# A two-layer mixture-of-experts trunk: expert rows added by gathers into SBUF in place of accumulating scatters into DRAM

## What is computed

```
x = _layer_norm(DEEPNORM_ALPHA * x + mixed, ln_g[l, 0], ln_b[l, 0])
x = _layer_norm(DEEPNORM_ALPHA * x + grouped_moe(x, w_router, b_router, w_e_in[l], w_e_out[l]),
                ln_g[l, 1], ln_b[l, 1])

def grouped_moe(x, ...):              # T = 1024 tokens of D = 1024
    expert, weight = two experts of each token, with weights that sum to 1
    order = jnp.argsort(flat_e)       # the 2048 (token, expert) pairs sorted by expert
    xs = xt[order // TOP_K]
    h_gate, h_up = jnp.split(lax.ragged_dot(xs, w_e_in, group_sizes), 2, axis=-1)
    y = lax.ragged_dot(jax.nn.silu(h_gate) * h_up, w_e_out, group_sizes)
    y = y * weight.reshape(-1)[order][:, None]
    out = jnp.zeros_like(xt).at[tok].add(y)
```

## Time and profile before

| | |
|---|---|
| median of 3 runs | 3053.19 us (3050.14 to 3059.01) |
| the profiled execution, its own time | 3060.01 us |
| its span | 3058.3 us |
| mean granted TensorE clock | 0.953 |
| busy PE / DVE / ACT / POOL | 91% / 51% / 38% / 10% of the span |
| DMA | 398.58 MB, mean 130 GB/s |

### The profile page before, as it was taken

The page is one execution under the profiler, slowest core; times in us unless marked ns, Lnnn a source line. Parts: engine busy times, 40 slices in busy tenths (PEclk is TensorE's granted clock), DMA queues, the critical chain, the costliest instruction groups (busy, mean ns, idle before and its releaser), DMA issues.

```text
span 3058.3 us, 47623 instructions
## 1 busy us (share of the span) xinstructions
PE 2796.5 (91%) x15876; PEld 1463.5 (48%) x15877; DVE 1561.2 (51%) x2494; ACT 1163.7 (38%) x1846; POOL 309.4 (10%) x240
## 2 busy tenths in 40 slices
PE   5999999999999599999579999999999995999994
PEld 3555554554444345454345555555544442454542
DVE  3243473343346667656633345634433466577665
ACT  3234413222222157655432444132222321577663
POOL 0000000000000023222310000000000000132323
PEclk8999999999999799999789999999999996999996
DMA  7200001111115389977722000111111154699974
GB/s 256 70 1 29 29 18 36 52 35 53 52 62 185 126 301 347 323 257 240 221 88 70 28 1 29 35 35 35 53 49 46 58 207 154 222 340 360 314 255 143
DMA packets 150903, 398.58 MB, mean 130 GB/s; under 512 B 13700, under 2 KB 58928, under 8 KB 149904
## 3 DMA queue, kind: packets, MB, share of 16 engines
q1 hardware_dynamic: 133104, 327.59, 29.5%
q0 software_dynamic: 14816, 54.12, 7.1%
q10 hardware_dynamic: 2816, 14.68, 1.3%
HBM read 343.91 MB, written 56.63 MB: 131 GB/s over the span
## 4 chain that ended last, share of the span: by engine, by line
PE 77%; DVE 6%; issue 6%; PEld 3%; DMA 3%; ACT 2%; DVEq 2%; SPq 1%; POOL 0%; PEldq 0%; ACTq 0%; POOLq 0%
PE PA L2031 15%; PE PA L1606 10%; PE PA L1608 10%; PE PA L1607 10%; PE PB L2050 7%; PE PC L1587 3%; PE PB L1608 3%; PE PB L1607 3%; PE PB L1606 3%; PE PD L1606 2%; PE PD L1608 1%; PE PD L1607 1%; DMA W<-in_w_in_dram 1%; PE PA L1704 1%; PEld PA L1606 1%
## 5 line engine op out<-in xcount | busy, mean ns | idle before, releaser
L2031 PE MATMUL PA<-XT,RA 128*128 128x512 f16 x2304 | 511.2, 382 | 9.6 <-DVE RA L1023 6.3
L1606 PE MATMUL PA<-XT,W 128*128 128x512 f16 x1216 | 461.7, 380 | 0.7 <-issue 0.7
L1607 PE MATMUL PA<-XT,W 128*128 128x512 f16 x1216 | 461.3, 379 | 0.0
L1608 PE MATMUL PA<-XT,W 128*128 128x512 f16 x1216 | 461.2, 379 | 0.0
L2031 PEld LDWEIGHTS PA<-XT,RA 128*128 128x128 f16 x2304 | 226.2, 98 | 276.9 <-issue 15.6
L1023 DVE SCALAR_TENSOR_TENSOR XT<-OT,XT 128x1024 f16<-128x1024 f32 x256 | 295.0, 1219 | 40.4 <-ACT XT L901 40.3
L1023 DVE SCALAR_TENSOR_TENSOR W<-W 128x512 f16<-128x512 f32 (+2 forms) x320 | 199.6, 660 | 167.3 <-ACT W L675 155.7
L825 ACT ACTIVATE WK<-PA,bT 128x512 f32<-128x512 f32 x128 | 87.9, 687 | 495.9 <-PE PA L1608 495.4
L2050 PE MATMUL PB<-W,WK 128*128 128x512 f16 x1152 | 260.8, 384 | 6.7 <-DVE W L1023 4.4
L901 ACT ACTIVATE XT<-OT 128x1024 f16<-128x1024 f32 x240 | 230.7, 1043 | 44.1 <-issue 40.9
L1252 DVE SCALAR_TENSOR_TENSOR MKV<-WK,PB 128x512 f32<-128x512 f32 x96 | 66.0, 688 | 339.2 <-PE PB L1608 339.2
(11 more groups left out here) (355 smaller groups left out, 4239.1 us busy)
## 6 DMA issues: line engine op xcount, KB each, us to landing
OT<-in_w_e_in_dram SPq DMA_DIRECT2D x256, 512.0 KB
RA<-in_w_e_out_dram SPq DMA_DIRECT2D x128, 512.0 KB
W<-in_w_in_dram SPq DMA_DIRECT2D x104, 512.0 KB, 4.7
W<-in_w_branch_dram SPq DMA_DIRECT2D x32, 256.0 KB, 4.9
W<-in_w_out_dram SPq DMA_DIRECT2D x16, 512.0 KB, 5.2
x_rows<-RC SPq DMA_DIRECT2D x16, 512.0 KB, 5.5
y_sum<-RC SPq DMA_DIRECT2D x16, 512.0 KB, 5.9
OT<-y_sum SPq DMA_DIRECT2D x16, 512.0 KB, 3.7
```

What stands on the lines that cost most here:

```text
L1606: mm(dst, lhs(0), rhs(0), start=first, stop=False)
L1607: mm(dst, lhs(0), rhs(1), start=False, stop=False)
L1608: return mm(dst, lhs(1), rhs(0), start=False, stop=last)
L2031: q = mm(PA[:, half, :], ROWS[:, a, k * P:(k + 1) * P], EIS[:, b, k, half * HALF:(half + 1) * HALF], start=k == 0 and a + b == 0, stop=k = ...
```

## The change

- y_sum goes. A DRAM tensor y_rows with one place per slot (32 tiles of 128 rows) takes its place. POOL stores each tile of YROW whole and plainly (store_tile), without a column of indices.
- SP no longer stores x1 into y_sum, and no longer loads x2 from it.
- x2 is now x1's own buffer (RC). After the last store has landed, POOL issues two indirect gathers with an add for each token tile, from y_rows into x2: the first expert's rows (j = 0) and the second's (j = 1), 16 in all. They go in the order of the loop shown below; the second of a tile waits until the first has landed. DVE waits for both.
- DVE keeps the slot numbers: one more copy of 16 columns into slot_row.
- At the start, ACT's queue fills y_rows' upper half with two copies of x (4 MB each), in place of 512 KB of zeros.

```diff
-        y_sum = dram("y_sum", [T + P, D])
+        y_rows = dram("y_rows", [TILES * P, D])
...
-        x2 = [OT[:, i * D:(i + 1) * D] for i in range(NT)]
+        x2 = [RC[:, i * D:(i + 1) * D] for i in range(NT)]
...
+        slot_row = BR[:, NT * P + 2 * TILES + 1:NT * P + 2 * TILES + 1 + 2 * NT].bitcast(U32)
...
+        y_tiles = y_rows.rearrange("(i r) n -> i r n", r=P)
...
                         sp.dma_start(x1_rows[(t - 3) * P:(t - 2) * P, :], X1[:, t - 3, :]).then_inc(x1_st, 16)
-                        sp.dma_start(y_sum[(t - 3) * P:(t - 2) * P, :], X1[:, t - 3, :]).then_inc(y_init, 16)
...
-                sp.wait_ge(y_st, (g0 + last + 1) * 16)
-                sp.sem_inc(passed, 1)
-                for t in range(NT):
-
-                    if t >= 4:
-                        sp.wait_ge(y_used, at(y_used, t - 3))
-                    sp.dma_start(x2[t], y_sum[t * P:(t + 1) * P, :]).then_inc(y_ld[t % 4], 16)
...
-                def add_rows(i):
+                def store_tile(i):
 
                     pool.wait_ge(y_ev, g0 + i + 2)
-                    nc.gpsimd.tensor_copy(at_row[:, 1:2], src_row[:, bass.ds(i, 1)]).then_inc(at_dst, 1)
-                    pool.wait_ge(at_dst, g0 + i + 1)
                     pool.sem_inc(passed, 1)
-                    nc.gpsimd.indirect_dma_start(y_sum, bass.IndirectOffsetOnAxis(at_row[:, 1:2], 0), YROW, None,
-                                                 compute_op=ALU.add).then_inc(y_st, 16)
+                    pool.dma_start(y_tiles[bass.ds(i, 1), :, :].rearrange("a r n -> (a r) n"), YROW).then_inc(y_st, 16)
+
+                def add_rows(t, j):
+                    here, before = y_add[t % (NT - 1)], 32 * (t // (NT - 1))
+                    if j == 1 or before:
+                        pool.wait_ge(here, at(here, before + 16 * j))
+                        pool.sem_inc(passed, 1)
+                    nc.gpsimd.indirect_dma_start(x2[t], None, y_rows, bass.IndirectOffsetOnAxis(slot_row[:, j * NT + t:j * NT + t + 1], 0),
+                                                 compute_op=ALU.add).then_inc(here, 16)
...
-                    add_rows(i - 1)
-                add_rows(before_last)
-                add_rows(last)
+                    store_tile(i - 1)
+                store_tile(before_last)
+                store_tile(last)
+                pool.wait_ge(y_st, (g0 + last + 1) * 16)
+                pool.sem_inc(passed, 1)
+                for t in range(NT + 2):
+                    if t < NT:
+                        add_rows(t, 0)
+                    if t >= 2:
+                        add_rows(t - 2, 1)
 
                 pool.wait_ge(ln2_ld, at(ln2_ld, 32))
                 for t in range(NT - 2):
...
             act.dma_start(x1_rows[T:T + P, :], zeros).then_inc(zero_st, 16)
-            act.dma_start(y_sum[T:T + P, :], zeros).then_inc(zero_st, 16)
+            act.dma_start(y_rows[2 * T:3 * T, :], x[0]).then_inc(zero_st, 16)
+            act.dma_start(y_rows[3 * T:4 * T, :], x[0]).then_inc(zero_st, 16)
...
+                nc.vector.tensor_copy(slot_row, gm[:, 0:2 * NT])
...
-                        v.wait_ge(y_ld[t % 4], at(y_ld[t % 4], 16 * (t // 4 + 1)))
+                        v.wait_ge(y_add[t % (NT - 1)], at(y_add[t % (NT - 1)], 32 * (t // (NT - 1) + 1)))
...
-                        v.sem_inc(y_used, 1)
```

More of the change, by code:

```diff
@@ L195, in trunk @@
         row_wt = BR[:, NT * P + TILES:NT * P + 2 * TILES]
-        at_row = BR[:, NT * P + 2 * TILES:NT * P + 2 * TILES + 2].bitcast(U32)
+        at_row = BR[:, NT * P + 2 * TILES:NT * P + 2 * TILES + 1].bitcast(U32)
+        slot_row = BR[:, NT * P + 2 * TILES + 1:NT * P + 2 * TILES + 1 + 2 * NT].bitcast(U32)
         PICK = BR[:, 0:NT * P].bitcast(F16).rearrange("p (a s) -> p a s", a=2 * NT)
@@ L235, in trunk @@
         x1_st = sem("x1_st", NT * 16)
-        y_init = sem("y_init", NT * 16)
         inv_a = sem("inv_a", 2)
@@ L240, in trunk @@
         at_src = sem("at_src")
-        at_dst = sem("at_dst")
         lb_ld = sem("lb_ld")
@@ L357, in trunk @@
         y_st = sem("y_st")
-        y_ld = [sem(f"y_ld{i}", 2 * 16) for i in range(4)]
-        y_used = sem("y_used", NT)
+        y_add = [sem(f"y_add{i}", (4 if i == 0 else 2) * 16) for i in range(NT - 1)]
         f_var = sem("f_var", NT)
@@ L598, in gather_tile @@
                     gather(at_row[:, 0:1])
-                def add_rows(i):
+                def store_tile(i):
                     pool.wait_ge(y_ev, g0 + i + 2)
-                    nc.gpsimd.tensor_copy(at_row[:, 1:2], src_row[:, bass.ds(i, 1)]).then_inc(at_dst, 1)
-                    pool.wait_ge(at_dst, g0 + i + 1)
                     pool.sem_inc(passed, 1)
-                    nc.gpsimd.indirect_dma_start(y_sum, bass.IndirectOffsetOnAxis(at_row[:, 1:2], 0), YROW, None,
-                                                 compute_op=ALU.add).then_inc(y_st, 16)
+                    pool.dma_start(y_tiles[bass.ds(i, 1), :, :].rearrange("a r n -> (a r) n"), YROW).then_inc(y_st, 16)
[6 more added lines that the diff above has]
+                                                 compute_op=ALU.add).then_inc(here, 16)
                 pool.wait_ge(x1_st, at(x1_st, NT * 16))
-                pool.wait_ge(zero_st, 32)
+                pool.wait_ge(zero_st, 48)
                 pool.wait_ge(inv_ok, at(inv_ok, 1))
@@ L614, in _ @@
                 pool.wait_ge(tab_ok, at(tab_ok, 1))
-                pool.wait_ge(y_init, at(y_init, NT * 16))
                 pool.sem_inc(passed, 1)
@@ L1132, in evict_half @@
                     if u == 4 and t == NT - 1:
-                        v.wait_ge(zero_st, 32)
+                        v.wait_ge(zero_st, 48)
                     evict_proj(j, RN[:, t, u % 2 * HALF:(u % 2 + 1) * HALF], C_RQ + u % 2 * HALF)
```

## The result

| | before | after |
|---|---|---|
| median | 3053.94 us (3050.14 to 3059.01) | 3126.47 us (3115.29 to 3133.85, 4 runs) |
| ratio, 95% interval | | 1.0233, 1.0199 to 1.0268 |
| the profiled execution, its span | 3060.01, 3058.3 us | 3125.36, 3123.8 us |
| mean granted TensorE clock | 0.953 | 0.943 |
| POOL busy | 309.4 us | 209.7 us |

The kernel became slower by 2.3%. The forecast was 3114 us, with a range of 3082 to 3140 and a chance of 0.97 for slower.

A forecast was written before the change was run, and what follows sets the result against it. PE's 16.85 us iteration bounds the expert loop, and each layer's last stage is all on the path. 25.9 + 33.9 + 0.9 + 0.3 = +61 us on the median 3053.2 gave 3114 us, range 3082 to 3140.

The forecast's parts named there:

- first gather to POOL free for the bias: Layer's last stage: data start, 13 gathers of 2.7 us, the semaphore and the last issue take 39.2 us.
- price of a gather with an add: Last stage: each queued gather costs 2.7 us, priced by the scatter with an add, which also reads two sources.
- first bias to the stage's end: Last stage behind the gathers: 5.3 us to the first low part, then 29.9 as before, together 35.2 us.
- the stage, layer 2: From layer 2's last eviction to DVE's last low part: 79.4 us in place of 53.5, +25.9.
- the stage, layer 1: The same stage in layer 1, where the next layer's weights also meet the gathers: +33.9 us.
- the weights' share of layer 1: The next layer's 4 MB of weights share the DMA engines with layer 1's gathers: +8 us.
- start: Kernel start: ACT issues two 4 MB copies in place of one store ahead of the first weights: +0.9 us.
- three signs of being wrong: Layer 2's first bias outside 30 to 50 us after last eviction; layer 1's stage not longer; PE's iteration changed.
- A: Last stage: the add into SBUF is as cheap as a plain gather; 3076 to 3109 us, chance 0.25.
- B: Last stage: the gather with an add is dearer, or POOL's issue bounds; beyond 3132 us, chance 0.11.
- C: Start: ACT's queue is held until the first 4 MB copy has moved; 3131 or 3148 us, chance 0.05.
- D: Expert loop: scatter waits do hold PE, so plain stores give back up to 83.5 us; 3030 us, chance 0.02.

The follow-up runs named there:

- experiment 1: The changed kernel with SP waiting for each layer's last gather before the next layer's first weights: 3120.41 us, ratio to before 1.0207.
- experiment 5: The kernel before with the two 4 MB copies of x into y_rows added at its start: 3058.85 us, ratio to before 0.9998.
- experiment 4: The kernel before with the add taken out of its scatters, so rows overwrite each other in y_sum: 3062.16 us, one run.
- experiment 2: The changed kernel with the add taken out of its 16 gathers, which overwrite x2: 3110.01 us, one run.
- experiment 3: The changed kernel with the last stage's bias on DVE in place of POOL: 3102.56 us, ratio to before 1.0144.
- experiment 6: The kernel before with POOL's biases waiting for DVE's next tile and the last scatter's index column copied early: 3049.14 us, ratio 0.9967.

## Why the prediction was right, step by step

The mechanism was the one forecast, and its terms came out as follows (layer 2 unless said).

| term | forecast, us | measured, us |
|---|---|---|
| last store, from issue to landing | 4.9 | 4.40 |
| eviction's end to first gather | 5.05 | 6.10 |
| first gather to POOL free for the bias | 39.2 | 40.73 |
| price of a gather with an add | 2.7 | 2.58 |
| first bias to the stage's end | 35.2 | 34.7 |
| the stage, layer 2 | +25.9 | +28.2 |
| the stage, layer 1 | +33.9 | +35.5 |
| the weights' share of layer 1 | 8 | 7.5 (experiment 1) |
| start | +0.9 | +0.7 in the chain; in the whole not to be told from zero (experiment 5) |
| scatters in the loop | 0 | 0 (experiment 4) |

None of the three signs of being wrong came: the first bias of layer 2 started 46.8 us after the last eviction (30 to 50 allowed), layer 1's stage is the longer one, and PE's iteration is unchanged.

**The price of the gather.** Taken from the scatter with an add, which reads two sources and writes one, at its best rate. The nearest row was the right one: 203 GB/s in the queue against the 209 of the earlier trace rows. What was too small is what I put around it. The last issue came 39.2 us after the first, and 13 x 2.58 = 33.5 of that are transfers, so the fixed part is 5.6 us, where I had put 2.8; and the chain has 0.7 us between the eviction and the store's issue and 1.0 between its landing and the first gather, where I had put 0.15 in all. With 0.12 us too much for each of the 13 gathers, 0.2 too little for the last issue, and 0.5 too much each for the store's landing and for the tail, that gives 2.1 of the 2.2 us by which layer 2 exceeds its term. The errors have both signs and in part cancel: the sum lacked 4.6 us and had 2.5 too much. That it came so close is to this extent luck.

**The bytes alone.** The prediction weighed the fit of the Trainium skill (DMA: Bandwidth & Descriptors, Anatomy of one DMA — SWDGE (gpsimd) path), which has no term for an add and would have given about 3075. The trace disagrees for a gather with an add: 2.58 us in the queue, where the estimate from the page's 436 GB/s is 1.2. Without the add experiment 2's fuller window gives 1.5.

**The fixed order behind the gathers.** From the first bias to the end 34.7 us, in place of 35.2: DVE's order forbids any cover, as forecast. One sign was wrong in its shape: I expected DVE to be idle for some 25 us before its first low part. It is idle for 29.5 us before its first moments, a few us between tiles, and 12.3 before the low part, since tile 0's second gather is only the fourth in the queue. Nothing hung on it.

**The weights.** I expected them on the queue at about 1495, some 3 us after the eviction. They came 4.8 us after it, and the interference was 7.5 us.

**The start.** ACT's two issues took 0.52 and 0.61 us, where the one store had 0.45. They are on the path, as forecast: in the chain, ACT's first split starts 2.06 us after the first weights have landed before, 2.78 after, and 3.38 in experiment 5, which keeps the store and adds both copies. The expected 40.2 for this split still came out as 37.95, since the first weights landed at 35.17 us in that execution and at 37.22 before. The landing differs by execution (35.39 in experiment 4, 34.78 in experiment 5), by more than the 0.7. "Nothing" for unit 2 was a near miss: its landing took 12.4 us after, against 3.5 before, and ACT waited 2.20 us for it. PE was busy for 34.66 of the 35 us from 65 to 100, so at most 0.3 us came of it; experiment 4, without copies, has the same 34.66.

**The median.** The sum, +61 us, is near the 65.4 us between the two profiled executions. The medians differ by 72.5. Against the median of before's 23 executions by the end of the experiments, 3059.06 us, after's 3126.47 is 67.4 more. The four executions of after spread over 18.6 us, and the interval of the ratio allows +61 to +82, so I can't say whether the last 7 us are more than spread.

**The rivals.** A (the add costs nothing) fell to the 203 GB/s; experiment 2 shows that even then the kernel is slower. B (dearer, or POOL's issue bounds) fell: 1.55 us for each issue, and POOL waited. The issue in layer 2 that ran beside DVE's subtract and multiply had begun 0.08 us ahead of it (3064.20) and took 1.55 too, so here DVE held none. C (ACT's queue held) fell: ACT's first split began at 37.95 us, right behind its issues. D (not slower) fell to PE's 16.85 us and to experiment 4.

## What to carry to other kernels

Before replacing an accumulating transfer, look at whether its waits reach the engine that bounds the loop; here 83.5 us of waits were worth nothing in the loop, and the add itself was worth 4 us in all, at the ends of the two layers. Price a new transfer by the nearest row with the same number of sources, not by its bytes, and ask what stands behind it on the queue that issues it: ten of the 28 us were in eight short operations that had to wait behind sixteen issues. When a last stage is short of engine time, two-input operations of DVE and POOL that start together are a place to look.

## What the runs showed that I had not expected

- The add makes the issue longer as well as the transfer: 1.54 us against 0.94 for a gather into SBUF, and 2713 against 2114 ns for the mean scatter in the loop.
- In experiment 3 three issues of layer 2's gathers began while DVE's addition with two SBUF inputs (1.22 us) was under way, and took 2.26 to 2.31 us in place of 1.54.
- The second gather with an add landed 7.01 us after its issue (the chain above), while a queued one costs 2.58. So a short run of such gathers costs more than their number times 2.58.
- Two copies of 4 MB from DRAM to DRAM beside PE's densest stretch, 35 us until they land, cost nothing that 10 runs could tell.
- Letting an engine start later made a kernel faster by 0.3%: the bias of experiment 6 waits longer than it must, and DVE gains more than POOL loses.
